# Softplus in one instruction, and the scores' PSUM reused for the weights, in a stick-breaking attention kernel

## The reference

```
z = einsum("bqhd,bkhd->bhqk", q, k) * HEAD_DIM ** -0.5
causal = k_pos[None, :] < q_pos[:, None]
log_keep = where(causal, log_sigmoid(-z), 0.0)
rev = cumsum(log_keep, axis=3, reverse=True)
after = concatenate([rev[..., 1:], zeros_like(rev[..., :1])], axis=-1)
w = where(causal, exp(log_sigmoid(z) + after), 0.0)
o = einsum("bhqk,bkhd->bqhd", w, v)
```

## Time and profile before

| | us |
|---|---|
| median of 2 runs | 5107.68 (5088.97 to 5126.4) |
| the profiled execution's own time | 4938.11 |
| its span (slowest core) | 4936.9 |
| PE busy | 3261.4 (66%) |
| ACT busy | 2473.9 (50%) |
| DVE busy | 2234.3 (45%) |
| cores, shortest and longest span | 4901.7 to 4936.9 |

### The profile page before, as it was taken

One profiled execution on the slowest core, in us unless ns is written; L12 is line 12 of the kernel. 1 busy time (PEld: TensorE's weight loads), 2 busy tenths in 40 slices (PEclk: granted clock), 3 DMA queues, 4 the chain that ended last, 5 costly groups with the idle time before them and its releaser, 6 DMA issues.

```text
span 4936.9 us, 52649 instructions; the slowest of 8 cores (4901.7 to 4936.9 us)
## 1 busy us (share of the span) xinstructions
PE 3261.4 (66%) x14892; PEld 1219.7 (25%) x15112; DVE 2234.3 (45%) x2974; ACT 2473.9 (50%) x3336; POOL 370.6 (8%) x497
## 2 busy tenths in 40 slices
PE   1435445445367888798878887988747488365684
PEld 1222222222142222122212221222123133132232
DVE  1455555555523556355544554455533323434234
ACT  1344444444435889579867887788811111011211
POOL 1000000000010000000000000000010022110221
PEclk9667677677655889679878888788968799677897
DMA  3111111111021000100010001000062333272432
GB/s 79 52 49 50 47 52 52 47 51 52 22 35 35 1 1 1 35 1 1 1 35 1 1 1 35 1 1 1 14 132 47 85 52 52 81 111 56 86 58 75
DMA packets 152777, 195.61 MB, mean 40 GB/s; under 512 B 90464, under 2 KB 110960, under 8 KB 152304
## 3 DMA queue, kind: packets, MB, share of 16 engines
q0 software_dynamic: 91184, 85.76, 10.0%
q1 hardware_dynamic: 61312, 106.48, 7.1%
HBM read 204.24 MB, written 48.00 MB: 51 GB/s over the span
## 4 chain that ended last, share of the span: by engine, by line
PE 55%; ACT 17%; DVE 11%; issue 7%; DMA 7%; POOL 1%; ACTq 0%; DVEq 0%; SPq 0%; POOLq 0%
PE pb L284 54%; ACT sb_wtp L261 9%; DVE sb_junk L274 2%; DVE sb_xsb L274 2%; PE pt L287 2%; ACT L261 2%; DMA sb_Vh<-V_d 2%; ACT sb_tq L261 2%; DVE sb_uc L274 1%; DMA sb_xt<-X_d 1%; ACT sb_stat L261 1%; DMA sb_W<-w_in 1%; DMA sb_xt<-xf 1%; DVE sb_rr L686 1%; DVE sb_gy L264 1%
## 5 line engine op out<-in xcount | busy, mean ns | idle before, releaser
L264 DVE TENSOR_TENSOR sb_S32p<-sb_S32p,sb_spp 128x1024 f32<-128x1024 f32 (+3 forms) x624 | 662.2, 1061 | 789.4 <-ACT sb_spp L261 785.6
L284 PE MATMUL pb<-sb_QT_all,sb_KTh 64*128 64x512 bf16 (+3 forms) x2560 | 764.2, 393 | 302.7 <-ACT sb_wtp L261 188.5
L287 PE MATMUL pt<-sb_ident,sb_xsb 128*128 128x128 bf16 x792 | 100.1, 306 | 984.1 <-DVE sb_xsb L274 984.1
L261 ACT ACTIVATE sb_wtp<-pb 128x1024 bf16<-128x1024 f32 (+3 forms) x640 | 573.5, 896 | 251.9 <-PE pb L284 228.4
L261 ACT ACTIVATE sb_spp<-sb_ep,sb_c_one 128x1024 bf16<-128x1024 f32 (+3 forms) x640 | 647.2, 1011 | 4.6
L261 ACT ACTIVATE sb_ep<-pb 128x1024 f32<-128x1024 f32 (+3 forms) x640 | 567.5, 887 | 148.5 <-PE pb L284 148.5
L284 PE MATMUL pb<-sb_Sbp,sb_nones 128*128 128x512 bf16 (+3 forms) x1244 | 494.6, 398 | 14.6 <-issue 13.7
L284 PE MATMUL pb<-sb_spp,sb_ntri 128*128 128x512 bf16 (+3 forms) x1188 | 469.0, 395 | 0.0
L284 PEld LDWEIGHTS pb<-sb_QT_all,sb_KTh 64*128 64x128 bf16 x2560 | 190.9, 95 | 985.2 <-issue 971.4
L281 DVE CAST sb_Sbp<-sb_S32p 128x1024 bf16<-128x1024 f32 (+3 forms) x624 | 381.8, 612 | 110.6 <-PE pb L284 83.0
L284 PE MATMUL pb<-sb_wtp,sb_Vh 128*64 128x512 bf16 (+3 forms) x1280 | 395.8, 397 | 12.0 <-ACT sb_wtp L261 11.5
(11 more groups left out here) (198 smaller groups left out, 3844.6 us busy)
## 6 DMA issues: line engine op xcount, KB each, us to landing
sb_xt<-xf SPq DMA_DIRECT2D x96, 512.0 KB, 3.5
sb_xt<-X_d SPq DMA_DIRECT2D x17, 512.0 KB, 4.1
KT_d<-sb_ktc POOLq DMA_DIRECT2D x16, 512.0 KB, 3.4
V_d<-sb_vc POOLq DMA_DIRECT2D x16, 512.0 KB, 3.8
sb_KTh<-KT_d SPq DMA_DIRECT2D x16, 512.0 KB, 5.0
sb_Vh<-V_d SPq DMA_DIRECT2D x16, 512.0 KB, 5.5
sb_wu<-w_up POOLq DMA_DIRECT2D x8, 1024.0 KB, 8.6
sb_wd<-w_dn POOLq DMA_DIRECT2D x8, 1024.0 KB, 11.1
```

Source lines behind the costliest of these rows:

```text
L261: S.op(act, lambda: nc.scalar.activation(out=out, in_=in_, func=func, **kw), reads, writes)
L264: S.op(q, lambda: q.eng.tensor_tensor(out=out, in0=in0, in1=in1, op=op), reads, writes)
L284: S.op(pe, lambda: nc.tensor.matmul(out, lhsT=lhsT, rhs=rhs, start=start, stop=stop, skip_group_check=skip), reads, writes)
L287: S.op(pe, lambda: nc.tensor.transpose(out=out, in_=in_, identity=ident[:]), reads + [R["const"]], writes)
```

## The change

p1a and p1b become qa and qb. The PSUM banks are no longer split into Zp and Wp: three pairs rotate over the units (pair k % 3). qa only computes z. qb takes Softplus of z from PSUM straight into spp, one activation in place of Exp and Ln. (With an environment variable it takes the old two; it isn't set.) qc adds the ntri and nones matmuls into the same pair in which z still stands, so z isn't computed a second time and the mask isn't added again. qd takes Exp of that pair, as p2b did. qe is p3 with its accumulators in the two PSUM tiles pt, since the three pairs are all in use. run_units has two units in flight behind the first where it had three: in round t there are qa of t, pcast of t-1, qb of t, qc and qd of t-1, qe of t-2. Stages 1 and 3 and the sample streams' attention stand as they were.

```diff
--- before.py
+++ after.py
@@ -771,12 +771,11 @@
         ep = Rot([sb(f"ep{i}", [128, 2, 512], F32, es3) for i in range(2)])
         spp = Rot([sb(f"spp{i}", [128, 2, 512], BF16, es3) for i in range(4)])
         wtp = Rot([sb(f"wtp{i}", [128, 2, 512], BF16, es3) for i in range(3)])
-        Zp, Zr = bigs[0], [banks.bufs[0][1], banks.bufs[1][1]]
-        Wp, Wr = bigs[1], [banks.bufs[2][1], banks.bufs[3][1]]
-        Ob = [banks.bufs[4][0], banks.bufs[5][0]]
-        Or = [banks.bufs[4][1], banks.bufs[5][1]]
-        Z3 = Zp[:, :].rearrange("p (a n) -> p a n", a=2)
-        W3 = Wp[:, :].rearrange("p (a n) -> p a n", a=2)
+        Bp = [bigs[i] for i in range(3)]
+        Br = [[banks.bufs[2 * i][1], banks.bufs[2 * i + 1][1]] for i in range(3)]
+        B3 = [Bp[i][:, :].rearrange("p (a n) -> p a n", a=2) for i in range(3)]
+        Ob = [pts.bufs[h2][0][:, :].bitcast(F32) for h2 in range(2)]
+        Or = [pts.bufs[h2][1] for h2 in range(2)]
 
         def make_units(kth, kth_r, vh, vh_r, hp, M):
             q_res = [R["QT", m] for m in range(4 * M, 4 * M + 4)]
@@ -793,29 +792,30 @@
                 units.append(dict(kT=[kth[hb:hb + 64, ft * 128:(ft + 1) * 128] for hb in (0, 64)],
                                   v=[vh[:, ft, hb:hb + 64] for hb in (0, 64)],
                                   qT=[QT_all[hb:hb + 64, hp, M * 512:(M + 1) * 512] for hb in (0, 64)], q_res=q_res,
-                                  res=[kth_r, vh_r], c_lo=c_lo, diag=diag, valid=(validt[:, ft:ft + 1] if ft < 3 else None), k=k,
-                                  first=(k == 0), last=(ft == 0),
+                                  res=[kth_r, vh_r], c_lo=c_lo, diag=diag, k=k, first=(k == 0), last=(ft == 0),
                                   out_ap=[OT_all[:, hp * 2 + h2, M * 512:(M + 1) * 512] for h2 in range(2)], out_res=o_res))
             return units
 
-        def p1a(u):
-            c0 = u["c_lo"]
+        def qa(u):
+            c0, k = u["c_lo"], u["k"]
+            B, Brr = Bp[k % 3], Br[k % 3]
             for h2 in range(2):
-                mm(Zp[:, h2 * 512 + c0:(h2 + 1) * 512], u["kT"][h2], u["qT"][h2][:, c0:512], True, True, u["res"] + u["q_res"],
-                   [Zr[h2]], skip=True)
+                mm(B[:, h2 * 512 + c0:(h2 + 1) * 512], u["kT"][h2], u["qT"][h2][:, c0:512], True, True, u["res"] + u["q_res"], [Brr[h2]],
+                   skip=True)
                 if u["diag"]:
                     d0, d1 = u["diag"]
-                    mm(Zp[:, h2 * 512 + d0:h2 * 512 + d1], ident[:, :], mneg[:, :], False, True, [C], [Zr[h2]], skip=True)
-            e, e_r = ep.next()
-            u["e"], u["e_r"] = e, e_r
-            act_fn(e[:, :, c0:512], Z3[:, :, c0:512], AF.Exp, Zr, [e_r])
-
-        def p1b(u):
-            c0 = u["c_lo"]
-            e, e_r = u["e"], u["e_r"]
+                    mm(B[:, h2 * 512 + d0:h2 * 512 + d1], ident[:, :], mneg[:, :], False, True, [C], [Brr[h2]], skip=True)
+
+        def qb(u):
+            c0, k = u["c_lo"], u["k"]
             spt, sp_r = spp.next()
             u["sp"], u["sp_r"] = spt, sp_r
-            act_fn(spt[:, :, c0:512], e[:, :, c0:512], AF.Ln, [e_r, C], [sp_r], bias=c_one[:, 0:1])
+            if os.environ.get("MK_NOSOFTPLUS"):
+                e, e_r = ep.next()
+                act_fn(e[:, :, c0:512], B3[k % 3][:, :, c0:512], AF.Exp, Br[k % 3], [e_r])
+                act_fn(spt[:, :, c0:512], e[:, :, c0:512], AF.Ln, [e_r, C], [sp_r], bias=c_one[:, 0:1])
+            else:
+                act_fn(spt[:, :, c0:512], B3[k % 3][:, :, c0:512], AF.Softplus, Br[k % 3], [sp_r])
             if not u["last"]:
                 tt(dve, S32p[:, :, c0:512], S32p[:, :, c0:512], spt[:, :, c0:512], ALU.add, [sp_r, S32r], [S32r])
 
@@ -824,27 +824,24 @@
                 c0, k = u["c_lo"], u["k"]
                 cp(dve, Sbp[k % 3][:, :, c0:512], S32p[:, :, c0:512], [S32r], [Sbr[k % 3]])
 
-        def p2a(u):
+        def qc(u):
             c0, k = u["c_lo"], u["k"]
+            B, Brr = Bp[k % 3], Br[k % 3]
             spt, sp_r = u["sp"], u["sp_r"]
             carry = not u["first"]
             for h2 in range(2):
-                o = Wp[:, h2 * 512 + c0:(h2 + 1) * 512]
-                mm(o, u["kT"][h2], u["qT"][h2][:, c0:512], True, False, u["res"] + u["q_res"], [Wr[h2]], skip=True)
-                if u["diag"]:
-                    d0, d1 = u["diag"]
-                    mm(Wp[:, h2 * 512 + d0:h2 * 512 + d1], ident[:, :], mneg[:, :], False, False, [C], [Wr[h2]], skip=True)
-                mm(o, ntri[:, :], spt[:, h2, c0:512], False, not carry, [sp_r, C], [Wr[h2]], skip=True)
+                o = B[:, h2 * 512 + c0:(h2 + 1) * 512]
+                mm(o, ntri[:, :], spt[:, h2, c0:512], False, not carry, [sp_r, C], [Brr[h2]], skip=True)
                 if carry:
-                    mm(o, nones[:, :], Sbp[(k - 1) % 3][:, h2, c0:512], False, True, [Sbr[(k - 1) % 3], C], [Wr[h2]], skip=True)
-
-        def p2b(u):
-            c0 = u["c_lo"]
+                    mm(o, nones[:, :], Sbp[(k - 1) % 3][:, h2, c0:512], False, True, [Sbr[(k - 1) % 3], C], [Brr[h2]], skip=True)
+
+        def qd(u):
+            c0, k = u["c_lo"], u["k"]
             wt, wt_r = wtp.next()
             u["w"], u["w_r"] = wt, wt_r
-            act_fn(wt[:, :, c0:512], W3[:, :, c0:512], AF.Exp, Wr, [wt_r])
-
-        def p3(u):
+            act_fn(wt[:, :, c0:512], B3[k % 3][:, :, c0:512], AF.Exp, Br[k % 3], [wt_r])
+
+        def qe(u):
             c0 = u["c_lo"]
             for h2 in range(2):
                 mm(Ob[h2][0:64, c0:512], u["v"][h2], u["w"][:, h2, c0:512], u["first"], u["last"], u["res"] + [u["w_r"]], [Or[h2]],
@@ -854,19 +851,18 @@
 
         def run_units(units):
             n = len(units)
-            for t in range(n + 3):
+            for t in range(n + 2):
                 if t < n:
-                    p1a(units[t])
-                if 0 <= t - 2 < n:
-                    p2a(units[t - 2])
+                    qa(units[t])
                 if 0 <= t - 1 < n:
                     pcast(units[t - 1])
+                if t < n:
+                    qb(units[t])
+                if 0 <= t - 1 < n:
+                    qc(units[t - 1])
+                    qd(units[t - 1])
                 if 0 <= t - 2 < n:
-                    p2b(units[t - 2])
-                if t < n:
-                    p1b(units[t])
-                if 0 <= t - 3 < n:
-                    p3(units[t - 3])
+                    qe(units[t - 2])
 
         for hp in range(4):
             kth, kth_r = KTh.next()
```

## The result

The changed kernel takes 5,783.4 us (median of 11 runs, 5,776.7 to 5,928.1); the kernel before takes 5,075.3 us (median of 10, 4,938.3 to 5,126.4). The ratio is 1.171, with a 95% interval of 1.167 to 1.175. The chip has a slower state in which a run takes some per cent longer; the kernel before was in it in most of its runs, and this ratio and all that follow are of undisturbed runs alone, here about 5,780 against 4,940 us.

A forecast was written before the change was run, and what follows sets the result against it. ACT was taken to pace the prompt's attention's wide units; 1628.6 us of loads, 1141.0 of activations and 91.4 of waits, less about 3, grow it by 809.5 to 5747.6; plus 137 gives 5,885 us, range 5,710 to 6,000.

The forecast's parts named there:

- the profiled execution: Whole program in the profiled run: 4938.1 us before plus 809.5 us growth of the prompt's attention gives 5747.6 us.
- Two tables, a load at each change of function: ACT in the prompt's attention: Softplus and Exp need different tables, so 1,248 added loads, 1,351 in all.
- 1.305 us a load: ACT, from one activation's end to the next's start across a table load; 1,248 of them make 1628.6 us.
- The 2.66 us a switch: Rival, load plus drain on ACT: 1,248 switches 3,320 us, time about 7,576 us; longer engine stops got chance 0.03.
- Softplus at the price of ep: ACT in the prompt's attention: Softplus costs as much as ep, 567.5 us for all 640 units.
- ACT waits for nothing within a call, and PE's clock doesn't matter: Prompt's attention: PE's 2.1 us and DVE's 1.92 us fit within ACT's 4.65 us a wide unit.
- The rival in which PE sets the pace: Wide units: at PE's lower clock 4.98 us exceeds ACT's 4.65, adding 148 us, 6,033 in all; chance 0.04.
- The stretch of 2,858 us: Prompt's attention after the change: 1628.6 loads, 1141.0 activations, 91.4 waits between calls, less about 3; before 2048.5 us.
- From the profiled execution to the median: Whole program: adds 137 us to 5747.6, the excess scaled to parts outside the prompt's attention, giving 5,885 us.
- the two runs' excess: Kernel before: the two runs' median of 5107.7 us lies 169.6 us above the profiled execution's 4938.1.
- The price of no loads: Prompt's attention without added loads: wide units save 417 us at 2.1 for 3.03, narrow ones 95; 4,426 us.
- The rival of a shared table: Softplus shares Exp's table, so no added loads in the prompt's attention: about 4,560 us, 11% faster; chance 0.05.

The follow-up runs named there:

- Experiments 1: Changed kernel with Exp then Ln in qb in place of Softplus, all else as changed: 4,805.6 us, ratio 0.963 to the kernel before.
- experiment 2: Changed kernel with Relu, which needs no other table, in place of Softplus: 4,283.0 us, ratio 0.859 to the kernel before.
- experiment 3: Changed kernel with Sigmoid, which needs another table than Exp, in place of Softplus: 5,783.3 us in one run.
- experiment 4: Kernel before with Softplus of z, written where Ln stood, in place of Exp and Ln; z still computed twice: 7,887.4 us, ratio 1.583.
- experiment 5: Kernel before with Softplus in place of Exp and Ln, written where Exp stood, ahead of the weights' Exp of unit t-2: 6,157.5 us.
- experiment 6: Kernel before with three rotating PSUM pairs and one z, keeping Exp, Ln, the old order and three units in flight: 4,705.5 us, ratio 0.944.

## Why the prediction was right, point by point

The forecast was 15% slower than the two runs' median; the ratio of the result is 1.171. The mechanism was right, and the sum for the profiled execution came within 1% of it.

- **Two tables, a load at each change of function.** Right: 1,351 loads, the very number forecast. Experiments 1 and 2 have 103 and no loss; experiment 3 has the 1,351 loads and the loss with another function. That Softplus and Exp are in no common table was the step that no row could show. The trace now agrees with the Trainium skill ("ScalarE: Activation LUTs", section "Table sets: the hidden batching unit"), which lists softplus in no set with exp.
- **1.305 us a load.** Right: from the end of one activation, 4390.39 + 1.02 = 4391.41, to the start of the next at 4392.73 are 1.32 us. The 2.66 us a switch of the Trainium skill ("ScalarE: Activation LUTs", section "What ACT_TABLE_LOAD costs") are not what this trace shows: by them, as an estimate, 1,248 switches would have cost 3,320 us, and the loads with their gaps took 1,637.
- **Softplus at the price of ep.** Right: 1024 ns against 1014; for all 640 units 571.8 us against the 567.5 taken.
- **ACT waits for nothing within a call, and PE's clock doesn't matter.** Right. The clock fell to its lower level, and a 512-column matmul took up to 0.63 us. That made PE 64% busy where I had expected near half, some 3.2 us a wide unit (13.68 us in 4380 to 4400, at a granted clock of 0.59) where I had 2.1; ACT is busy 2,745 of 2,910 us all the same. The rival in which PE sets the pace didn't come about. Experiments 4 and 5 show how near it lay: with two fixed pairs and the second z, ACT waits 3.71 us a unit for PE, or 0.94 in the units at the lower clock. My argument rested on the pair coming free two rounds ahead. No run separates that from the z that isn't computed again: without the two z of experiment 5's six matmuls the rest would take about 2.0 us (an estimate, 3.05 less 2 x 0.52 from the starts in its timeline), which fits under ACT's 2.3.
- **The stretch of 2,858 us.** 2,881 measured, made of 1,601.2 of loads, 1,143.7 of activations, some 36 of short gaps around the loads and 100.7 of waits for PE (123.8 less the 23.1 before the first load). Against the sum the loads with their gaps are 8 us longer, the waits at the calls' heads 9, the activations 3, and the 3 taken off for overlap weren't there.
- **The profiled execution.** 5,747.6 forecast, 5,795.8 measured. Of the 48 us, 23 are those of the stretch, and some 23 lie in stage 3, which took 1,390 us from the attention's end where it had 1,367. Those are spread between cores: in one execution stage 3 takes 1,340 to 1,375 us on the eight cores of the kernel before and 1,344 to 1,391 on those of the changed one, whose page is that of the core with the longest. Between the medians of the cores lie 6 us.
- **From the profiled execution to the median.** This step failed. It carried 137 us of the two runs' excess over to the changed kernel. In the later runs it is no property of the program: the changed kernel's median is 5,783, 12 us under its profiled execution, and before's shortest runs are at 4,938 to 4,944. It sat in the yardstick too: against a median of 5,108 the forecast gave 15%, and the undisturbed ratio is 17%. Without the step the forecast would have been 36 us too low, with it it was 102 too high. The range held both.
- **The price of no loads.** The rival of a shared table gave 4,426 us before that step, 512 us saved; the profiled execution of experiment 2, which is that case, took 4,276, 662 saved. I priced a wide unit at PE's 2.1 us; DVE's chain set 2.19. Both parts of the sum were too small all the same. In the timelines of the calls the narrow units went from 469 to 287 us, 182 saved where I had PE's fifth, 95. The wide ones went from 1,488 to 1,006, 481 saved where I had 417. I had taken all 448 at the steady 3.03 us, and before they take 3.32 on average, since the first of each call are longer.

## What to carry to other kernels

Count the changes of function on ScalarE in the order in which it executes, and not the activations: a fused function saves one activation of 1.0 us a wide unit and here bought two loads of 1.3. If the fused function is wanted all the same, batch it, and look which engine's chain a longer batch exposes. And take a change apart: here one half alone was 5% faster than before (experiment 6), the other alone 58% slower (experiment 4), and their sum, 17% slower, told neither.

## What the runs showed of the hardware

- An activation's recorded length depends on what stands ahead of it. In the head-to-tail piece of experiment 6 ep takes 1.25 us in the rows and wtp 1.26, where both took 1.01 to 1.02 in the earlier trace rows, and yet they start only 0.91 us apart. There spacing, and not length, tells what an activation costs.
- A table load doesn't overlap its neighbours at all: it lasts 1.283 us, and the changed kernel has 1.32 us from the end of one activation to the start of the next. Two neighbouring activations can overlap by about 0.1 us: 0.92 us from wtp to spp at a length of 1.02.
- A table load stands behind the wait of the activation that needs it. It isn't done ahead: in experiment 4 ACT waits 3.71 us for PE, then loads for 1.28, then takes the Exp.
- PE's granted clock was at 0.50 in most of the changed kernel's attention (0.55 on average, PE busy 1,865 of 2,910 us), and at 1.00 in the steady piece of before (PE busy 26.05 of 30.30 us). It cost time where ACT waited for PE, as in experiment 5.
